# A two-block transformer kernel: the convolution's inputs projected first, all its taps on VectorE, and the modulation matmuls shifted by one iteration

## The reference

```
m  = silu(c) @ ada_w[i] + ada_b[i]                     # six modulation rows of 1024
hn = rms_norm(x) * (1 + scale) + shift
proj = hn @ ev_w_in                                    # q 512 | keys, values 256 | u 512 | gate 512
q, k = rope(rms_norm(q)), rope(rms_norm(k))            # 8 query heads, 2 key heads of 64
k, v = concat(keys, values of ctx (not rotated), own)  # 512 keys
attn = softmax(q k / 8) v
g = depthwise_conv(u * sigmoid(gate), 31 taps) + b     # 512 channels
g = silu(layer_norm(g))
h = x + m[2] * (concat(attn, g) @ ev_w_out)
```

## Time and profile before

| | |
|---|---|
| runs | 1767.9, 1754.98, 1755.61 us (median 1755.61) |
| the profiled execution | 1768.46 us, span 1766.7 us |
| TensorE matmul busy | 1339.0 us, 76% |
| VectorE, ScalarE, GpSimd busy | 492.0, 347.5, 152.1 us |
| memory read | 557.69 MB, 317 GB/s over the span |
| granted TensorE clock, mean | 0.867 of full speed |

### The profile page before, as it was taken

How to read it: one execution, slowest core, us unless ns; L and a number is a source line. 1 busy time by engine, 2 the same in 40 slices (tenths; PEclk the granted TensorE clock), 3 DMA queues, 4 the chain that set the end, 5 groups by cost and what they waited for, 6 DMA issues and landing times.

```text
span 1766.7 us, 18071 instructions
## 1 busy us (share of the span) xinstructions
PE 1339.0 (76%) x7746; PEld 785.0 (44%) x7746; DVE 492.0 (28%) x706; ACT 347.5 (20%) x513; POOL 152.1 (9%) x142
## 2 busy tenths in 40 slices
PE   5989875685675785599666657556568989899999
PEld 2744541231231231199411212112116857789997
DVE  1369540010100000356401001001006632445553
ACT  1111420010010010133100000000005632444442
POOL 1043000000000000100000000000004150440000
PEclk9999978898887897799788888778869966999999
DMA  9999749999999999984399999999998511435530
GB/s 372 394 388 356 296 158 423 417 412 422 417 421 422 413 420 422 401 306 170 128 422 422 422 422 421 422 422 422 423 391 300 190 48 64 161 109 183 183 112 25
DMA packets 110000, 561.83 MB, mean 318 GB/s; under 512 B 8516, under 2 KB 9908, under 8 KB 54126
## 3 DMA queue, kind: packets, MB, share of 16 engines
q1 hardware_dynamic: 105880, 551.76, 77.7%
q0 software_dynamic: 2208, 8.36, 1.3%
q10 hardware_dynamic: 1846, 0.75, 0.2%
HBM read 557.69 MB, written 3.16 MB: 317 GB/s over the span
## 4 chain that ended last, share of the span: by engine, by line
PE 40%; DMA 31%; DVE 3%; ACT 2%; SPq 1%; issue 1%; POOL 0%; DVEq 0%; ACTq 0%; POOLq 0%
PE ps L1855 22%; DMA ring<-in_moe_w_down 13%; DMA ring<-in_moe_w_up 12%; PE ps L2105 8%; DMA ring<-in_moe_w_gate 5%; PE ps L1840 3%; PE ps L2119 1%; SPq L472 1%; PE ps L2339 1%; DMA ring<-in_w_in 1%; PE ps L2152 1%; PE ps L2354 0%; PE ps L2327 0%; PE ps L2329 0%; ACT ring_parts L587 0%
## 5 line engine op out<-in xcount | busy, mean ns | idle before, releaser
L2105 PE MATMUL ps<-ring,scratch 128*32 128x512 f32 x3072 | 469.7, 768 | 284.1 <-DMA ring<-in_moe_w_up 129.1
L2105 PEld LDWEIGHTS ps<-ring,scratch 128*32 128x32 f32 x3072 | 127.1, 136 | 601.0 <-issue 598.4
L1855 PE MATMUL ps<-ring_parts,scratch_parts 128*128 128x512 f32 x656 | 190.8, 410 | 5.1 <-DVE xT_parts L1163 1.4
L1855 PE MATMUL ps<-scratch_parts,ring_parts 128*128 128x256 f32 x704 | 145.7, 282 | 0.0
L1855 PEld LDWEIGHTS ps<-ring_parts,scratch_parts 128*128 128x128 f32 x656 | 125.2, 193 | 38.3 <-issue 7.4
L587 ACT ACTIVATE ring_parts<-ring 128x2048 fp32r<-128x2048 f32 x56 | 106.1, 1919 | 93.7 <-PE ps L1855 87.4
L1855 PEld LDWEIGHTS ps<-scratch_parts,ring_parts 128*128 128x128 f32 x704 | 115.9, 190 | 0.3
L438 DVE TENSOR_TENSOR ring_parts<-ring,ring_parts 128x2048 fp32r<-128x2048 f32 x44 | 100.7, 2289 | 53.4 <-ACT ring_parts L587 52.1
L1456 DVE TENSOR_TENSOR scratch<-ps,gate_bc 128x512 f32<-128x512 f32 x16 | 10.3, 686 | 298.2 <-PE ps L2105 298.2
L1448 DVE TENSOR_TENSOR scratch<-scratch,ps 128x1024 f32<-128x1024 f32 x8 | 9.8, 1222 | 286.7 <-PE ps L2105 286.7
L1855 PE MATMUL ps<-xT_parts,ring_parts 128*128 128x256 f32 x288 | 80.9, 281 | 1.3 <-DVE xT_parts L1154 1.3
(11 more groups left out here) (379 smaller groups left out, 1559.8 us busy)
## 6 DMA issues: line engine op xcount, KB each, us to landing
ring<-in_moe_w_gate SPq DMA_DIRECT2D x64, 2048.0 KB, 28.6
ring<-in_moe_w_up SPq DMA_DIRECT2D x64, 2048.0 KB, 25.8
ring<-in_moe_w_down SPq DMA_DIRECT2D x64, 2048.0 KB, 31.6
ring<-in_ada_w SPq DMA_DIRECT2D x24, 2048.0 KB, 12.9
ring<-in_mlp_w SPq DMA_DIRECT2D x16, 2048.0 KB, 8.3
ring<-in_sc_w_in SPq DMA_DIRECT2D x6, 2048.0 KB, 20.9
ring<-in_w_in SPq DMA_DIRECT2D x6, 2048.0 KB, 16.9
ring<-in_xattn_wkv SPq DMA_DIRECT2D x4, 2048.0 KB, 29.8
```

The source lines that it names most:

```text
L1855: last = mm(out, lhs[x], rhs[y], start=start and n == 0, stop=stop and n == 2)
L2105: last = mm(ps[32 * j:32 * j + 32, banks[half], :], src[:, k, CAP * j:CAP * (j + 1)], w[j * RUN // EG][:, j % (EG // RUN), col:col + 512], ...
```

## The change

It moves work of the first block and changes no arithmetic but the order in which one channel tile's taps are added.

- `STREAM` now has `ev_u`, `ev_gate`, `ev_q`, `ev_kv`, and then all four chunks of group 1 together. SyncE issues them in this order, the context rows between `ev_q` and `ev_kv`.
- TensorE projects `ev_u`, transposes the convolution's parameters (now into bank 2), projects `ev_gate` and `ev_q`, transposes the context, projects keys and values, and takes the four chunks of group 1 behind them.
- VectorE writes `gpad` early and does 35 taps (`TAPS_Q`) while `ev_q` is projected, writes its half of the context columns, and does 12 more (`TAPS_KV`). The other 77 stand in the loop, 8 an iteration (n = 0 to 9).
- GpSimd's 19 taps and `pool_taps` are gone; all 124 are VectorE's.
- The norms of the heads come in two steps: the ten heads of queries and own keys, rotation, then the two context key heads. ScalarE takes a root for each.
- In the loop the chunks of a group are taken at n % 4 = 1, 2 and 3 (two chunks at 3), none at n % 4 = 0. `ada_rows` stands behind the taps of n = 4, 8, 12, `mod_cols` at n = 5, 9, 13 ahead of the taps. `LN_AT` is 10.

```
-STREAM = [("ada0a", 4), ("ev_q", 1), ("ev_kv", 1), ("ev_u", 1), ("ada0b", 2), ("ev_gate", 1),
-          ("ada0b_rest", 2), ("ada0c", 4), ...
+STREAM = [("ada0a", 4), ("ev_u", 1), ("ev_gate", 1), ("ev_q", 1), ("ev_kv", 1), ("ada0b", 4),
+          ("ada0c", 4), ...
...
-        POOL_TAPS = 19
-        LN_AT = 12
+        LN_AT = 10
+        TAPS_Q, TAPS_KV, TAPS_LOOP = 35, 12, 8
...
@@ scalar @@
-            transposed("ctx", cT)
...
+            whole(act, "ev_gate")
+            for j in range(2):
+                nc.scalar.activation(flat(sg[:, 2 * j:2 * j + 2, :]), pb(6 + j), ACT.Sigmoid).then_inc(sem("cv_gate"), 1)
+
             whole(act, "ev_q")
...
-            whole(act, "ev_kv")
+            transposed("ctx", cT)
             for w, bank in ((0, 2), (1, 3)):
+                if w:
+                    whole(act, "ev_kv")
+                else:
+                    act.wait_ge(sem("own_kv"), 1)
...
+                if not w:
+                    act.wait_ge(sem("inverses"), 1)
+                    nc.scalar.activation(sm[:, 24:44], sm[:, 24:44], ACT.Sqrt).then_inc(sem("roots"), 1)
+            act.wait_ge(sem("inverses"), 2)
+            nc.scalar.activation(sm[:, 44:48], sm[:, 44:48], ACT.Sqrt).then_inc(sem("roots"), 1)
...
@@ gpsimd @@
-            for k in range(CONVK - POOL_TAPS, CONVK):
-                dst = cpool if k == CONVK - POOL_TAPS else lnrow[:, :]
-                link(nc.gpsimd.tensor_scalar(dst, gpad[:, c, k:k + N], cw[:, c, k:k + 1], None, ALU.mult))
-                if k > CONVK - POOL_TAPS:
-                    last = nc.gpsimd.tensor_tensor(cpool, cpool, lnrow[:, :], ALU.add)
...
@@ vector @@
-            taps_left = [(k, c) for k in range(CONVK) for c in range(CT) if c < CT - 1 or k < CONVK - POOL_TAPS]
+            taps_left = [(k, c) for k in range(CONVK) for c in range(CT)]
...
+            taps(TAPS_Q)
+            transposed("ctx", cT)
+            taps(TAPS_KV)
...
+            head_norms(6, 0, 10, sq, 0)
...
+            head_norms(10, 10, 12, sq_ctx, 20)
...
             for n in range(NT * NQ):
...
+                if n % 4 == 1 and n > 1:
+                    mod_cols(1 + n // 4, 3)
+                taps(TAPS_LOOP)
                 if n % 4 == 0 and n:
                     ada_rows(1 + n // 4, 3)
-                taps(9)
-                if n == LN_AT - 1:
-                    pool_taps()
-                if n % 4 == 0 and n:
-                    mod_cols(1 + n // 4, 3)
...
@@ tensor @@
+            pe.wait_ge(sem("gpad"), 2)
+            pe.wait_ge(sem("cv_gate"), 2)
             transposes("ctx", ctx_rows)
...
-                if n % 4 == 0:
+                if n % 4 == 1:
                     pe.wait_ge(sem("mod_cols"), 2 + n // 4)
-                ada(2 + n // 4, n % 4, 3)
+                for c in ((), (0,), (1,), (2, 3))[n % 4]:
+                    ada(2 + n // 4, c, 3)
```

More of the change, by code:

```diff
@@ L489, in _ @@
             evw = a["ev_w_in"][0]
+            columns("ev_u", evw, 1, col0=768)
+            columns("ev_gate", evw, 1, col0=1280)
             columns("ev_q", evw, 1)
@@ L492, in _ @@
             columns("ev_kv", evw, 1, width=256, col0=512)
-            columns("ev_u", evw, 1, col0=768)
-            modulations(1, (0, 1))
-            columns("ev_gate", evw, 1, col0=1280)
-            modulations(1, (2, 3))
-            for g in range(2, len(ADA)):
+            for g in range(1, len(ADA)):
                 modulations(g)
@@ L1310, in attn_rows @@
+            head_norms(10, 10, 12, sq_ctx, 20)
+            for t in range(NT):
+                head_gains(t, 10, 12, 1).then_inc(sem("ev_rope"), 1)
+            ada_rows(1, 3)
+            dve.wait_ge(sem("ev_qkT_ps"), 2)
+            nc.vector.tensor_copy(kT, pb(2)).then_inc(sem("ev_kT"), 1)
+            mod_cols(1, 3)
             def attn_rows(t):
@@ L1926, in _ @@
             normed_columns("x")
-            i = FIRST["ev_q"]
-            arrived(pe, i)
-            used(to_rows(i, xT, (0, 1)))
             def kv_rows(bank, lhs):
@@ L1938, in kv_rows @@
                 return last
+            i = FIRST["ev_u"]
+            arrived(pe, i)
+            used(to_columns(i, xT, (4, 5)))
+            pe.wait_ge(sem("params_in"), PARAMS * 16)
+            for c in range(CT):
+                last = nc.tensor.transpose(ps[:, 2, 34 * c:34 * c + 34], cwrow[0:34, P * c:P * (c + 1)], ident[0:34, 0:34])
+            last.then_inc(sem("cw_ps"), 1)
+            i = FIRST["ev_gate"]
+            arrived(pe, i)
+            used(to_columns(i, xT, (6, 7)))
+            i = FIRST["ev_q"]
+            arrived(pe, i)
+            used(to_rows(i, xT, (0, 1)))
+            pe.wait_ge(sem("gpad"), 2)
+            pe.wait_ge(sem("cv_gate"), 2)
             transposes("ctx", ctx_rows)
             arrived(pe, FIRST["ev_kv"])
-            kv_rows(2, xT)
+            pe.wait_ge(sem("cw"), 1)
+            kv_rows(2, xT).then_inc(sem("own_kv"), 1)
             normed_columns("ctx")
             used(kv_rows(3, cT))
-            pe.wait_ge(sem("params_in"), PARAMS * 16)
-            for c in range(CT):
-                last = nc.tensor.transpose(ps[:, 4, 34 * c:34 * c + 34], cwrow[0:34, P * c:P * (c + 1)], ident[0:34, 0:34])
-            last.then_inc(sem("cw_ps"), 1)
-            pe.wait_ge(sem("cw"), 1)
-            for name, banks in (("ev_u", (4, 5)), ("ev_gate", (6, 7))):
-                i = FIRST[name]
-                arrived(pe, i)
-                used(to_columns(i, xT, banks))
-                pe.wait_ge(sem("ev_rows"), 10)
-                for c in range(2):
-                    ada(1, (2 if name == "ev_gate" else 0) + c, 3)
+            pe.wait_ge(sem("ev_rows"), 10)
+            for c in range(4):
+                ada(1, c, 3)
             pe.wait_ge(sem("ev_rope"), 4)
@@ L1964, in _ @@
             last.then_inc(sem("ev_qkT_ps"), 1)
+            pe.wait_ge(sem("ev_rope"), 6)
             for s in range(4):
```

107 lines of the change are left out of this document (44 added, 63 removed).

## The result

The changed kernel took 1751.26 us in the median of 20 runs (1743.51 to 1759.49), the kernel before 1768.06 us in 20 runs beside it (1754.5 to 1777.84). The ratio is 0.9919 with a 95% interval of 0.9896 to 0.9943: 0.81% faster, 0.57 to 1.04%. The forecast was 1742.1 us from a median of 1755.61, a gain of 13.5 us or 0.77%, and "within 1%" had most of the chance. So the share came out as forecast, and the absolute time is 9.2 us above the forecast, because the median of before in 20 runs lies 12.45 us above that of the three it started from. The profiled execution took 1744.99 us (span 1743.2) against 1768.46 (1766.7).

The account below looks back on a forecast made before the run. VectorE, then TensorE, bounded the loop; after the change TensorE nearly throughout. Start 108.1, work 75.0 and waits 3.1 end the values at 186.2 us instead of 199.7, so 1755.61 - 13.5 = 1742.1 us; whole range 1734 to 1756.

Parts of the forecast that it names:

- within 1%: Whole kernel: the outcome that the time differs from before by less than 1% (17.6 us), given a chance of 0.70.
- TensorE's sum: Ahead of the loop: TensorE's reordered projections, transposes and four chunks added up, ending at 103.1 us.
- The rival of the high price: Taps stay at 0.608 us without GpSimd, so loop starts 7.6 us later; 6 us slower, 1761.6 us; chance 0.05.
- The 75.0 us of work: Loop: TensorE's work from its first transposes to its last values, without the waits.
- 2.4 forecast at n = 1: Loop start: TensorE waits 2.4 us for maximum 1, as no chunk stands between the transposes at n = 0.
- 0.7 for the root: Loop: the layer norm's root holds up the exponentials once, taken as 0.7 us, between 0 and 2.5.
- Half clock in the loop: Rival: TensorE's clock falls for 10 us in the loop, losing 4 to 5 us; 1747 us; chance 0.16.
- a sign of being wrong: Loop: the clock falling there was listed as showing the forecast wrong; it expected clock 1.00.
- What follows costs nothing: Behind the loop: attention rows, transposes and output projection keep their order and distances, costed at nothing.
- a rival with the other sign: From 200.70 to 253.00 us: less time at lower clock gains about 4 to 6 us more, 1737 us; chance 0.14.
- The last of my signs: Behind the first block: the forecast is wrong if the shift at 253 us is not that at the end.
- the forecast's own range: Whole kernel: 1737 to 1748 us, from the unknown loop start (-0.3 to +3) and root (0 to 2.5).

Follow-up runs that it names:

- e2: Changed kernel with 19 taps of tile 3 given back to GpSimd, beside the early taps and head norms; profiled at 1764.76 us.
- e8: Changed kernel with only the layer norm moved, to n = 12 instead of 10; profiled at 1769.43 us.
- e6: Changed kernel with the loop's first group of chunks taken one an iteration at n = 0 to 3; profiled at 1739.03 us.
- e7: Same as e6, with the loop's taps also spread 2, 6, 8, 8, 8, then 9 an iteration; median 1748.0 us, ratio 0.9875 to the kernel before.
- e5: Kernel before with GpSimd's 19 taps moved to VectorE, 11 an iteration, layer norm still at n = 12; profiled at 1770.15 us.
- e9: Kernel before with the layer norm at n = 10 and VectorE's taps 11 an iteration, GpSimd keeping its 19; profiled at 1780.62 us.
- e1: Changed kernel with 19 taps of tile 3 given back to GpSimd, beside the loop; profiled at 1765.24 us.
- e3: Changed kernel with no early taps, all 124 in the loop at 11 an iteration, layer norm at n = 12; profiled at 1761.51 us.
- e4: Changed kernel with the loop's modulation chunks, row copies and column reads at their old places, one chunk every iteration; profiled at 1747.48 us.
- e10: Kernel before with all 124 taps on VectorE, 13 an iteration, and the layer norm at n = 10; profiled at 1777.78 us.
- e11: The same kernel as e6, run again; median of six runs 1752.7 us, ratio 0.9895 to the kernel before.

## Why the prediction was right, and where it was not

*Ahead of the loop.* The steps of TensorE's sum hold within 1.3 us: `ev_gate` ends at 64.5 (63.2, because the first projection of the row now takes 15.70 us and not 14.08), the context's keys and values at 93.8 (94.3), the four chunks at 102.6 (103.1). `gpad` is written at 65.25 (65.2), the head norms start at 87.7 (88.1), the loop at 104.92 (105.4). That 47 taps lie in idle time is shown by the wait of 0.86 us left behind them.

*The price of a tap.* 0.405 us throughout; e2 shows that GpSimd's work, and not the place, sets 0.627. The rival of the high price is refuted. What GpSimd's taps add is not spread evenly over VectorE's (e2).

*TensorE as the bound of the loop.* The 75.0 us of work were the right size: from the first transposes (107.61) to the last values (186.77) are 79.16 us, of which 2.06 + 0.22 are waits and about 2.3 the lower clock behind the first of them (0.45 in the transposes, 0.81 in the values, 1.09 in the chunk), which leaves 74.6.

*The waits.* 2.4 forecast at n = 1, 2.06 measured; 0.7 for the root, 0.22 measured. Both sizes were estimates, and the second rested on the two chunks beside the root, which e8 confirms.

*Half clock in the loop.* I had held it apart, at a chance of 0.16 and 4 to 5 us, and had named it as a sign of being wrong. It came, at the wait I had named, but for 6.8 us of time, and cost 2.3. Rival and forecast were both partly true. The smaller waits and the earlier start paid for it: 12.93 us gained at the marker against 13.5.

*"What follows costs nothing."* This step failed. 2.8 us of the 12.9 were gone at the last expert combination, 1.8 of them before the first expert product. The lower level around the router lasted 27.3 us without a break after, and 3.4 and then 17.1 us before. Over all profiles the time from the last values to the last combination goes with the length of the long piece: 1130.3 or 1130.4 us at 17.1 (before, e2, e6, e7), 1131.8 and 1132.3 at 23.9 (e5, e9), 1133.1 to 1135.0 at 27.3 (the changed kernel, e1, e3, e4, e8, e10, e11). e6 and e11, one kernel, show 17.1 and 27.3. So this is no fixed cost of the change; whether the change makes the long one likelier is open. I had it as a rival with the other sign. The last of my signs came with it: the shift at the first expert product (11.1 us) is not that at the end (23.5 us).

*The gain in time.* 10.1 us at the last combination, 10.1 / 1766.7 = 0.57%, is what the profiles show of the change. The runs say 0.81%, with 0.57 at the edge of the interval. A reading that fits is the late stretch. It makes 13.3 us between executions of one kernel, and the 20 runs of each kernel leave a gap of that kind: behind the six of before up to 1756.93, and behind the ten of the changed kernel up to 1748.44. The medians of these six and these ten are 1755.6 and 1745.9, 9.7 us or 0.55% apart, near the marker's 10.1. Six against ten then shift the medians of all runs further. The mean granted clock, which is on record for every run of the changed kernel, agrees: 30.7 us more at the lower level take 0.009 off it, and it is 0.870 to 0.877 in the ten up to 1748.44 and 0.863 to 0.869 in the others. Where a run had its stretches is on record for profiled ones only, and whether six against ten is chance is open. So the forecast's share came close partly by luck: too large by what was lost behind the loop, and met by how the runs happened to fall. Its starting point, 1755.61, was one of the six, which is why the absolute time lies above the forecast's own range of 1737 to 1748, though inside the whole one of 1734 to 1756.

*Where the gain comes from.* I had put it down to TensorE's work and had cost the norm's place only as a wait of 0.7. Three runs part the 13.1 us by which the loop is shorter: all taps on VectorE bring 0.7 (94.98 to e5's 94.29), the early taps (with the new order ahead of the loop) and the norm at n = 10 together bring 10.9 (to e4's 83.39), the shifted chunks 1.5 (to 81.85). In the kernel before, GpSimd's part and the norm's place with its denser taps bring nothing or lose: 0.7 us in the loop (e5), -10 at the marker (e9), both -5.3 (e10). Early taps alone and shifted chunks alone were not run there. Taken out of the changed kernel one at a time, GpSimd's part is worth 5.5, the norm's place 9.2 and the chunks 0.9; the early taps are worth 5.8 with the norm at n = 12. These add up to more than 12.9, so they are no separate shares. The norm's 9.2 is the price of an iteration without a chunk under it, which only the shifted chunks make: e3's loop, with shifted chunks and the norm at 12, is 3.0 us longer than e5's with old ones, while with the norm at 10 the shift gains 1.5. How the 10.9 divide between early taps and norm is open.

## What to carry to other kernels

Work that makes the other engines wait on one another, here a layer norm whose square and root hold up the exponentials, belongs where the bounding engine has independent work beside it. Moving either one without the other can cost most of what the change brings: 9.2 of 12.9 us for the norm over an emptied iteration. A wait of 2 us on TensorE can (e8, the changed kernel), though it need not (e4), cost as much again by the clock, so one independent chunk put in front of it can pay twice. And read a gain of under 1% at markers just behind the change, in several profiles, before believing the end of the span.
